# Two transformer blocks on one core: the mixer's head scores issued in pairs, and its remainders as two products

## The chip, the cores and the metric

The kernel runs on one core of a Trainium2 chip. The metric is the device time of one execution in microseconds (us); lower is better. A measurement of this kernel is taken in several runs, and the median is compared.

## What is computed

The reference runs two transformer blocks over 256 tokens of width 1024 in float32. The first block (two layers of differential attention, a Fourier mixer and a gated feed-forward) is untouched. The second block has a feed-forward, then a *mixer*, then another feed-forward. The change lies in the mixer's attention, which is a "stick breaking" attention with 8 heads of width 64:

```python
z = jnp.einsum('bhqd,bhkd->bhqk', q_blk, k_c) * scale
valid = s_pos[None, :] < t_pos[:, None]
sp = jnp.where(valid, jax.nn.softplus(z), 0.0)
rem = lax.cumsum(sp, axis=3, reverse=True) - sp
log_a = jax.nn.log_sigmoid(z) - rem
a = jnp.where(valid, jnp.exp(log_a), 0.0)
outs.append(jnp.einsum('bhqk,bhkd->bhqd', a, v_c))
```

So for each head there are scores `z`, a softplus of them, a "remainder" (a sum over all later keys, made here as a product with a triangle of ones), an exponential, and the product with the values.

## The kernel before

All weights come from memory as a stream of chunks of 128 x 2048 float32 (1 MB). The chunks go through three slots. ScalarE (ACT) rounds a chunk to its high part (`split` in its program, L850), VectorE (DVE) subtracts to get the low part (`split` there, L1195, which signals `lo_ready`), and TensorE (PE) multiplies: each float32 product is three products of high and low parts (L438). In the mixer a projection chunk is 48 such matmuls of 256 columns; `projection(..., ks=range(4 * part, 4 * part + 4))` does one half of a chunk, 24 matmuls.

Each engine runs its own program strictly in the order in which it is written, and waits on semaphores. The order is written by hand. The attention of the mixer is woven into projection chunks 6 to 12. On PE, after each half chunk comes one step for one head: `remainders(h - 2)`, `z_scores(h)`, `values2(h - 4)`. Scores and keys lie with keys on the partitions, 384 columns for each head (256 queries against the first 128 keys, then 128 queries against the second 128 keys). The queries and keys of an even head lie on partitions 0 to 63 and those of the odd head on 64 to 127, so that a score product uses only 64 rows of PE's array (a row group).

For one head the work goes round the engines:

- PE `z_scores(h)` writes the scores to bank 2 or 3 (`z_done`). It waits for `z_read` of head h - 2, which frees the bank.
- ACT `log1p_exp(h)`: Abs (L1127), Exp (L1129) and Ln (L1131) of 128x384. Exp and Ln need different tables, and each change is a table load.
- DVE `softplus(h)`: three operations of 128x384 (L1567, L1571, L1574). The second signals `z_read`, the third `masked_ready`.
- PE `remainders(h)` (waits for `masked_ready`), then DVE `subtract_remainder(h)` (L1580, signals `log_a_ready`), ACT `exp_a(h)` (L1135), DVE `mask_a(h)` (L1585, signals `a2_ready`), and PE `values2(h)` (L782, L784).

ACT and DVE walk through steps `s` = 0 to 12. Before, step s holds the softplus chain of head s - 1 and the exponential of head s - 3. Odd steps also hold the split of chunk 9 + s // 2 and, on DVE, the copy of a finished projection out of its bank (L1626) or a convolution.

Of the kernel before, what the change touches and what calls it, by code (L numbers as in the profile page):

```python
# [30 lines left out]
P = 128  # L31
S = 256
# [3 lines left out]
HEADS = 8  # L36
ATT = 512
HD = 32
VD = 64
# [38 lines left out]
def fused_blocks(nc, x, stream, ada, w_f, layer_params, common_params, rows, consts32, out):  # L78
    with ExitStack() as ctx:
        def sb(name, shape, dt=F32):  # L80
            return ctx.enter_context(nc.sbuf_tensor(name, shape, dt))

        def sem(name):
            return ctx.enter_context(nc.semaphore(name))
# [5 lines left out]
        h = sb("h", [P, 2, D])  # L90
# [26 lines left out]
        def view(n, **dims):  # L117
            at = used[0]
            used[0] += n
            assert used[0] <= WORK  # L120
            return work[:, at:at + n]
# [7 lines left out]
        qT = view(4 * S).rearrange("p (k n) -> p k n", k=4)  # L129
        kT = view(4 * S).rearrange("p (k n) -> p k n", k=4)  # L130
# [30 lines left out]
        tri = c32[:, TRI:TRI + P]  # L161
        ones = c32[:, ONES:ONES + P]
# [22 lines left out]
        B = [banks[:, i, :] for i in range(8)]  # L185
# [87 lines left out]
        z_done = sem("z_done")  # L273
# [3 lines left out]
        z_read = sem("z_read")  # L277
# [152 lines left out]
        def _(pe):  # L430
# [320 lines left out]
            t = MIX_T  # L751
            EV = 8 * DEPTH

            def z_scores(h):

                if h >= 2:
                    pe.wait_ge(z_read, h - 1)
                r = VD * (h % 2)
                q, k = qT[r:r + VD, h // 2, :], kT[r:r + VD, h // 2, :]
                bank = B[2 + h % 2]  # L760
                nc.tensor.matmul(bank[:, 0:S], k[:, 0:P], q, start=True, stop=True, skip_group_check=True)
                nc.tensor.matmul(bank[:, S:S + P], k[:, P:S], q[:, P:S], start=False, stop=True,
                                 skip_group_check=True).then_inc(z_done, 1)

            def remainders(h):

                pe.wait_ge(masked_ready, h + 1)
                if h >= 2:
                    pe.wait_ge(log_a_ready, h - 1)
                bank, sp_ = B[4 + h % 2], soft[h % 3]  # L770
                nc.tensor.matmul(bank[:, 0:S], tri, sp_[:, 0:S], start=True, stop=False, skip_group_check=True)
                nc.tensor.matmul(bank[:, P:S], ones, sp_[:, S:S + P], start=False, stop=True, skip_group_check=True)
                nc.tensor.matmul(bank[:, S:S + P], tri, sp_[:, S:S + P], start=False, stop=True,
                                 skip_group_check=True).then_inc(rem_done, 1)

            def values2(h):
# [13 lines left out]
            for j in range(2, 20):  # L790

                if j < 12:
                    pe.wait_ge(proj_evac, EV + j - 1)
                elif 12 <= j < 14:
                    pe.wait_ge(cx_evac, j - 11)
                elif j >= 14:
                    pe.wait_ge(proj_evac, EV + j - 3)
                if j < 6 or j >= 13:
                    projection(t, j, B[j % 2], x_hi, x_lo)
                    continue  # L800
                for part in range(2):
                    h = 2 * (j - 6) + part
                    projection(t, j, B[j % 2], x_hi, x_lo, ks=range(4 * part, 4 * part + 4))
                    if h == 0:
                        pe.wait_ge(proj_evac, EV + 6)
                    if 2 <= h < HEADS + 2:
                        remainders(h - 2)
                    if h < HEADS:
                        z_scores(h)
                    if 4 <= h < HEADS + 3:  # L810
                        values2(h - 4)
                    if h == HEADS + 4:
                        values2(HEADS - 1)
# [30 lines left out]
        def _(act):  # L844
# [260 lines left out]
            for j in range(6):  # L1105
                act.wait_ge(chunk_done, 3 * t + j + 1)
                bank = B[j % 2][:, :].rearrange("p (m n) -> p m n", m=2)
# [13 lines left out]
            def log1p_exp(h):  # L1121

                act.wait_ge(z_done, h + 1)
                if h >= 2:
                    act.wait_ge(z_read, h - 1)
                buf = remain[:, h % 2, :]
                nc.scalar.activation(buf, B[2 + h % 2][:, 0:384], ACT.Abs).then_inc(soft_step, 1)  # L1127
                act.wait_ge(soft_step, 3 * h + 1)
                nc.scalar.activation(buf, buf, ACT.Exp, scale=-1.0).then_inc(soft_step, 1)  # L1129
                act.wait_ge(soft_step, 3 * h + 2)  # L1130
                nc.scalar.activation(buf, buf, ACT.Ln, bias=1.0).then_inc(soft_step, 1)  # L1131
# [11 lines left out]
                nc.scalar.activation(mix_hi[:, 4 + n, :], conv_y[:, n, :], ACT.Copy).then_inc(conv_hi, 1)  # L1143

            for s in range(13):
                if 1 <= s <= HEADS:
                    log1p_exp(s - 1)
                if 3 <= s < HEADS + 3:
                    exp_a(s - 3)
                if s >= 6 and s % 2 == 0:  # L1150
                    heads_hi((s - 6) // 2)
                if s % 2 == 1:
                    split(t, 6 + s // 2 + 3)
# [37 lines left out]
        def _(dve):  # L1191
            def split(t, j):

                dve.wait_ge(hi_ready, 3 * t + (j + 1))
                nc.vector.tensor_tensor(w_lo[j % SLOTS][:, :], raw[j % SLOTS][:, :],  # L1195
                                        w_hi[j % SLOTS][:, :].bitcast(F32), ALU.subtract).then_inc(lo_ready, 1)
# [364 lines left out]
            def softplus(h):  # L1561

                dve.wait_ge(soft_step, 3 * h + 3)
                if h >= 3:
                    dve.wait_ge(rem_done, h - 2)
                z, small_log = B[2 + h % 2][:, 0:384], remain[:, h % 2, :]
                nc.vector.scalar_tensor_tensor(soft[h % 3], z, 0.0, small_log, ALU.max, ALU.add)\  # L1567
                    .then_inc(soft_raw, 1)
                if h >= 4:
                    dve.wait_ge(o2_done, h - 3)  # L1570
                nc.vector.scalar_tensor_tensor(log_a[:, h % 4, :], z, 0.0, small_log, ALU.min, ALU.subtract)\  # L1571
                    .then_inc(z_read, 1)
                dve.wait_ge(soft_raw, h + 1)
                nc.vector.tensor_tensor(soft[h % 3], soft[h % 3], mask, ALU.mult)\  # L1574
                    .then_inc(masked_ready, 1)
# [16 lines left out]
            def conv(i):  # L1592

                dve.wait_ge(chunk_done, 3 * t + 11 + i)
                dve.wait_ge(proj_evac, 8 * DEPTH + 10)
                nc.vector.tensor_tensor(vpad[:, 2 * i:2 * i + 2, 2:S + 2],
                                        B[i][:, :].rearrange("p (m n) -> p m n", m=2), gate_c[:, 2 * i:2 * i + 2, :],
                                        ALU.mult).then_inc(cx_evac, 1)
                dve.wait_ge(cx_evac, i + 1)
                dve.wait_ge(pads_ready, 1)  # L1600
                for n in (2 * i, 2 * i + 1):
                    y = conv_y[:, n, :]
                    tap = [cp[:, CONV_W + 4 * w + n:CONV_W + 4 * w + n + 1] for w in range(3)]
                    nc.vector.tensor_scalar(y, vpad[:, n, 0:S], tap[0], None, ALU.mult).then_inc(conv_step, 1)
                    for w in (1, 2):
                        dve.wait_ge(conv_step, 4 * n + w)
                        nc.vector.scalar_tensor_tensor(y, vpad[:, n, w:w + S], tap[w], y, ALU.mult, ALU.add)\
                            .then_inc(conv_step, 1)
                    dve.wait_ge(conv_step, 4 * n + 3)
                    nc.vector.tensor_tensor(y, y, gate_b[:, n, :], ALU.mult).then_inc(conv_step, 1)  # L1610

            for s in range(13):
                if 3 <= s < HEADS + 3:
                    subtract_remainder(s - 3)
                if 1 <= s <= HEADS:
                    softplus(s - 1)
                if 3 <= s < HEADS + 3:
                    mask_a(s - 3)
                if s >= 6 and s % 2 == 0:
                    heads_lo((s - 6) // 2)  # L1620
                if s % 2 == 1:
                    j = 6 + s // 2
                    if j < 10:
                        dve.wait_ge(chunk_done, 3 * t + j + 1)
                        out = (gate_b if j < 8 else gate_c)[:, 2 * (j % 2):2 * (j % 2) + 2, :]
                        nc.vector.tensor_copy(out, B[j % 2][:, :].rearrange("p (m n) -> p m n", m=2))\  # L1626
                            .then_inc(proj_evac, 1)
                    else:
                        conv(j - 10)
                    split(t, j + 3)  # L1630
            for n in range(4):
                dve.wait_ge(conv_hi, n + 1)
# [165 lines left out]
```

## Time and profile before

| | |
|---|---|
| median of 3 runs | 1209.72 us (1205.0 to 1209.92) |
| the profiled execution's own time | 1209.38 us |
| its span, first to last instruction | 1207.7 us |
| mean granted clock of TensorE | 0.983 of full speed |
| PE busy | 1168.7 us, 97% |
| DVE busy | 865.5 us, 72% |
| ACT busy | 611.1 us, 51% |

The span is what the trace covers; the execution's own time is 1.7 us longer. Busy shares are averages over the whole program. The mixer's heads take up only the stretch from about 858 to 916 us, and that stretch has to be read by itself. A float32 product of the heads shows as two records of the same matmul (two passes); a product of high and low parts shows as one. Times in a row are given as start and duration, and neighbouring operations overlap by some 0.1 us, so that costs are best read as the distance between starts.

### The profile page before, as it was taken

The numbers are of one execution on the slowest core, as the hardware profiler recorded it, in microseconds if no ns is written. First come the engines' busy times: TensorE is split into PE (matmuls) and PEld (weight loads), VectorE is DVE, ScalarE is ACT, GpSimd is POOL, SyncE is SP. The second block draws the span as 40 slices with busy tenths as digits, with TensorE's granted clock in tenths as the row PEclk, the third lists the DMA queues.
The fourth block names the chain that finished last, engine by engine and source line by source line (L and its number), as shares of the span: only waits on it lengthen the run. The fifth ranks groups of instructions, "written<-read, shape, count | busy, mean of one in ns | idle before, by whom it ended". The sixth has DMA issues, their size and how long they took to land.

```text
span 1207.7 us, 17757 instructions
## 1 busy us (share of the span) xinstructions
PE 1168.7 (97%) x6642; PEld 1007.3 (83%) x6642; DVE 865.5 (72%) x1130; ACT 611.1 (51%) x745; POOL 104.7 (9%) x99
## 2 busy tenths in 40 slices
PE   8998999999999899999979999999999999999997
PEld 7987888887897788888768888878989987888886
DVE  6576878887857787888796788876477367655555
ACT  5674545444557454544444445444795445444443
POOL 2500600000130060000010000000000000000000
PEclk9999999999899999999989999998999998999999
DMA  9612676775342267777546677635424553555550
GB/s 362 238 71 105 229 271 263 298 279 225 139 176 70 105 238 269 263 290 282 222 142 212 255 278 282 264 150 180 170 101 143 177 185 134 201 175 187 195 174 35
DMA packets 34991, 242.62 MB, mean 201 GB/s; under 512 B 3808, under 2 KB 5232, under 8 KB 8448
## 3 DMA queue, kind: packets, MB, share of 16 engines
q1 hardware_dynamic: 28992, 196.56, 43.7%
q0 software_dynamic: 5520, 45.17, 10.2%
q8 instruction: 33, 0.54, 0.2%
q10 hardware_dynamic: 432, 0.24, 0.1%
q14 instruction: 14, 0.11, 0.0%
HBM read 240.90 MB, written 1.05 MB: 200 GB/s over the span
## 4 chain that ended last, share of the span: by engine, by line
PE 83%; DVE 8%; ACT 5%; issue 3%; DMA 0%; POOL 0%; DVEq 0%; SPq 0%; ACTq 0%
PE bank L438 39%; PE bank L471 25%; PE bank L473 13%; ACT w_hi L850 2%; PE bank L625 1%; DVE work L1328 1%; PE bank L602 1%; DVE small L1220 1%; PE bank L578 1%; DVE h L1233 1%; PE bank L615 1%; PE bank L528 1%; PE bank L643 1%; DVE w_lo L1195 0%; DVE h L1253 0%
## 5 line engine op out<-in xcount | busy, mean ns | idle before, releaser
L1195 DVE TENSOR_TENSOR w_lo<-raw,w_hi 128x2048 fp32r<-128x2048 f32 x178 | 414.4, 2330 | 141.4 <-ACT w_hi L850 141.3
L471 PE MATMUL bank<-x_parts,w_hi 128*128 128x512 f32 x1408 | 501.0, 400 | 2.7 <-DVE x_parts L1277 2.3
L473 PE MATMUL bank<-x_parts,w_lo 128*128 128x256 f32 x1408 | 396.2, 281 | 0.0
L850 ACT ACTIVATE w_hi<-raw 128x2048 fp32r<-128x2048 f32 x183 | 349.1, 1908 | 43.3 <-PE bank L438 37.3
L471 PEld LDWEIGHTS bank<-x_parts,w_hi 128*128 128x128 f32 x1408 | 265.7, 189 | 69.7 <-issue 3.5
L473 PEld LDWEIGHTS bank<-x_parts,w_lo 128*128 128x128 f32 x1408 | 267.2, 190 | 1.4
L438 PE MATMUL bank<-x_parts,w_hi 128*128 128x256 f32 x832 | 153.0, 286 | 0.7 <-ACT work L1111 0.7
L438 PE MATMUL bank<-w_hi,hid_hi 128*128 128x512 f32 x352 | 139.3, 396 | 2.8 <-DVE hid_lo L1316 2.8
L438 PE MATMUL bank<-w_lo,hid_hi 128*128 128x512 f32 x352 | 139.1, 395 | 0.0
L438 PE MATMUL bank<-w_hi,hid_lo 128*128 128x512 f32 x352 | 138.8, 394 | 0.0
L438 PEld LDWEIGHTS bank<-x_parts,w_hi 128*128 128x128 f32 x832 | 129.3, 191 | 3.8 <-issue 2.0
L438 PE MATMUL bank<-x_parts,w_lo 128*128 128x256 f32 x416 | 117.5, 283 | 0.0
L1328 DVE SCALAR_TENSOR_TENSOR work<-work,c_act 128x384 f32 x168 | 104.0, 619 | 5.9
L890 ACT ACTIVATE hid_hi<-work 128x512 fp32r<-128x512 f32 x44 | 27.8, 631 | 128.7 <-PE bank L438 114.7
L874 ACT ACTIVATE work<-bank 128x512 f32<-128x512 f32 x44 | 26.3, 598 | 125.7 <-PE bank L473 122.1
L438 PEld LDWEIGHTS bank<-w_hi,hid_hi 128*128 128x128 f32 x352 | 66.0, 187 | 20.0 <-DVE hid_lo L1316 4.1
L438 PEld LDWEIGHTS bank<-x_parts,w_lo 128*128 128x128 f32 x416 | 79.6, 191 | 0.0
L438 PEld LDWEIGHTS bank<-w_hi,hid_lo 128*128 128x128 f32 x352 | 66.0, 187 | 16.0
L438 PEld LDWEIGHTS bank<-w_lo,hid_hi 128*128 128x128 f32 x352 | 66.0, 188 | 14.2
L1316 DVE TENSOR_TENSOR hid_lo<-work,hid_hi 128x512 fp32r<-128x512 f32 x44 | 32.7, 743 | 59.3 <-ACT hid_hi L890 59.3
L438 PE MATMUL bank<-w_hi,x_parts 128*128 128x512 f32 x224 | 72.2, 399 | 2.6 <-DVE x_parts L1277 1.8
L356 POOL TENSOR_TENSOR small<-small 128x1 f32<-128x1 f32 x18 | 11.7, 652 | 532.9 <-DVE small L1259 421.7
(176 smaller groups left out, 1251.7 us busy)
## 6 DMA issues: line engine op xcount, KB each, us to landing
raw<-stream SPq DMA_DIRECT2D x183, 1024.0 KB, 4.8
work<-ada POOLq DMA_DIRECT2D x24, 1536.0 KB, 6.8
gain_rows<-rows POOLq DMA_DIRECT2D x11, 512.0 KB, 5.7
gate_rows<-rows POOLq DMA_DIRECT2D x3, 512.0 KB, 17.5
h<-x SPq DMA_DIRECT2D x4, 256.0 KB, 4.7
raw<-stream SPq DMA_DIRECT2D x2, 512.0 KB, 6.8
out<-z SPq DMA_DIRECT2D x4, 256.0 KB, 2.1
c<-consts SPq DMA_DIRECT2D x1, 962.0 KB, 13.9
```

The lines of the kernel that those rows point to most:

```text
L438: last = nc.tensor.matmul(out, stationary, moving, start=start and i == 0, stop=stop and i == 2, skip_group_check=True)
L471: nc.tensor.matmul(pair[:, n, :], wh[:, k, cols], x_parts[:, k, :, :].rearrange("p a n -> p (a n)"), start=k == 0, stop=False, skip_group_ ...
L473: last = nc.tensor.matmul(pair[:, n, 0:S], wl[:, k, cols], x_hi[:, k, :], start=False, stop=k == KT - 1, skip_group_check=True)
L528: last = nc.tensor.transpose(XT[k // 2][:, k % 2 * S + m * P:k % 2 * S + (m + 1) * P], z[:, m, k * P:(k + 1) * P], ident)
L578: last = nc.tensor.matmul(B[1][:, q:q + 1], ada_acc[:, q * P:(q + 1) * P], ones[:, 0:1], start=True, stop=True, skip_group_check=True)
L602: last = nc.tensor.matmul(SCORES[u][:, m * S:(m + 1) * S], qT[r:r + HD, p, m * P:(m + 1) * P], kT[r:r + HD, p, :], start=True, stop=True, ...
L850: nc.scalar.activation(w_hi[j % SLOTS][:, :], raw[j % SLOTS][:, :], ACT.Copy).then_inc(hi_ready, 1)
L874: nc.scalar.activation(gate_rest.rearrange("p (a n) -> p a n", a=2), GATE[:, :, S:2 * S], ACT.Copy)\
L890: nc.scalar.activation(out[:, :, :].rearrange("p k n -> p (k n)"), hidden, ACT.Copy)\
L1195: nc.vector.tensor_tensor(w_lo[j % SLOTS][:, :], raw[j % SLOTS][:, :], w_hi[j % SLOTS][:, :].bitcast(F32), ALU.subtract).then_inc(lo_ready, 1)
L1316: nc.vector.tensor_tensor(lo[:, :, :].rearrange("p k n -> p (k n)"), hidden, hi[:, :, :].rearrange("p k n -> p (k n)").bitcast(F32), ALU.s ...
L1328: nc.vector.scalar_tensor_tensor(acc, ada_raw[:, k, :], c_act[:, k:k + 1], acc, ALU.mult, ALU.add).then_inc(ada_step, 1)
```

## The change

On PE the scores of heads 2p and 2p + 1 are issued together after the first half of a chunk, in the order: even head 256 columns, odd head 256 columns, even head 128, odd head 128. The pair waits for `z_read` of both heads of the pair before it. After the second half of a chunk no scores are issued. The three products of a remainder (256, 128 and 128 columns) become two (384 and 128 columns). ACT runs the Abs, Exp and Ln of both heads of a pair one after the other in odd steps, and nothing of them in even steps. DVE does the softplus of the even head where it stood in odd steps, and that of the odd head at the end of the same step, just ahead of the split.

```diff
-            def z_scores(h):
-
-                if h >= 2:
-                    pe.wait_ge(z_read, h - 1)
-                r = VD * (h % 2)
-                q, k = qT[r:r + VD, h // 2, :], kT[r:r + VD, h // 2, :]
-                bank = B[2 + h % 2]
-                nc.tensor.matmul(bank[:, 0:S], k[:, 0:P], q, start=True, stop=True, skip_group_check=True)
-                nc.tensor.matmul(bank[:, S:S + P], k[:, P:S], q[:, P:S], start=False, stop=True,
-                                 skip_group_check=True).then_inc(z_done, 1)
+            def z_scores(pair):
+
+                if pair >= 1:
+                    pe.wait_ge(z_read, 2 * pair)
+                q, k = ([part[VD * u:VD * (u + 1), pair, :] for u in range(2)] for part in (qT, kT))
+                for u in range(2):
+                    nc.tensor.matmul(B[2 + u][:, 0:S], k[u][:, 0:P], q[u], start=True, stop=True,
+                                     skip_group_check=True)
+                for u in range(2):
+                    nc.tensor.matmul(B[2 + u][:, S:S + P], k[u][:, P:S], q[u][:, P:S], start=False, stop=True,
+                                     skip_group_check=True).then_inc(z_done, 1)
...
-                nc.tensor.matmul(bank[:, 0:S], tri, sp_[:, 0:S], start=True, stop=False, skip_group_check=True)
-                nc.tensor.matmul(bank[:, P:S], ones, sp_[:, S:S + P], start=False, stop=True, skip_group_check=True)
-                nc.tensor.matmul(bank[:, S:S + P], tri, sp_[:, S:S + P], start=False, stop=True,
+                nc.tensor.matmul(bank[:, 0:S + P], tri, sp_[:, 0:S + P], start=True, stop=False, skip_group_check=True)
+                nc.tensor.matmul(bank[:, P:S], ones, sp_[:, S:S + P], start=False, stop=True,
                                  skip_group_check=True).then_inc(rem_done, 1)
...
-                    if h < HEADS:
-                        z_scores(h)
+                    if h < HEADS and part == 0:
+                        z_scores(h // 2)
...
             for s in range(13):
-                if 1 <= s <= HEADS:
+                if s % 2 == 1 and s < HEADS:
                     log1p_exp(s - 1)
+                    log1p_exp(s)
...
                 if 3 <= s < HEADS + 3:
                     subtract_remainder(s - 3)
-                if 1 <= s <= HEADS:
+                if s % 2 == 1 and s < HEADS:
                     softplus(s - 1)
...
                     else:
                         conv(j - 10)
+                    if s < HEADS:
+                        softplus(s)
                     split(t, j + 3)
```

On VectorE, the place is step 5 of its walk. Before, the rows run from the softplus of head 4, over the mask of head 2, the copy of chunk 8 and the split of chunk 11, to the remainder of head 3 and the softplus of head 5 in step 6:

```order
L1567 SCALAR_TENSOR_TENSOR work<-bank,work 128x384 [waits rem_done,soft_step]
L1571 SCALAR_TENSOR_TENSOR work<-bank,work 128x384 [waits o2_done]
L1574 TENSOR_TENSOR work<-work,c 128x384 [waits soft_raw]
L1585 TENSOR_TENSOR work<-work,c 128x384 [waits a_exp_ready]
L1626 COPY work<-bank 128x512 [waits chunk_done]
L1195 TENSOR_TENSOR w_lo<-raw,w_hi 128x2048 [waits hi_ready]
L1580 TENSOR_TENSOR work<-work,bank 128x384 [waits z_read,rem_done]
L1567 SCALAR_TENSOR_TENSOR work<-bank,work 128x384 [waits rem_done,soft_step]
L1571 SCALAR_TENSOR_TENSOR work<-bank,work 128x384 [waits o2_done]
L1574 TENSOR_TENSOR work<-work,c 128x384 [waits soft_raw]
```

After, the same place (line numbers are one higher here):

```order
L1568 SCALAR_TENSOR_TENSOR work<-bank,work 128x384 [waits rem_done,soft_step]
L1572 SCALAR_TENSOR_TENSOR work<-bank,work 128x384 [waits o2_done]
L1575 TENSOR_TENSOR work<-work,c 128x384 [waits soft_raw]
L1586 TENSOR_TENSOR work<-work,c 128x384 [waits a_exp_ready]
L1627 COPY work<-bank 128x512 [waits chunk_done]
L1568 SCALAR_TENSOR_TENSOR work<-bank,work 128x384 [waits rem_done,soft_step]
L1572 SCALAR_TENSOR_TENSOR work<-bank,work 128x384 [waits o2_done]
L1575 TENSOR_TENSOR work<-work,c 128x384 [waits soft_raw]
L1196 TENSOR_TENSOR w_lo<-raw,w_hi 128x2048 [waits hi_ready]
L1581 TENSOR_TENSOR work<-work,bank 128x384 [waits z_read,rem_done]
```

The odd head's three operations moved from behind the split and the subtraction to a place ahead of both, but behind the mask of an older head.

On ScalarE, the place is the same pair of heads. Before, from the exponential of head 1 over the logarithm chain of head 4, the exponential of head 2 and the split to the chain of head 5:

```order
L1135 ACTIVATE work<-work 128x384 [waits log_a_ready]
L1127 ACTIVATE work<-bank 128x384 [waits z_read,z_done]
L1129 ACTIVATE work<-work 128x384 [waits soft_step]
L1131 ACT_TABLE_LOAD
L1131 ACTIVATE work<-work 128x384 [waits soft_step]
L1135 ACT_TABLE_LOAD
L1135 ACTIVATE work<-work 128x384 [waits log_a_ready]
L850 ACTIVATE w_hi<-raw 128x2048 [waits chunk_done,raw_landed2]
L1127 ACTIVATE work<-bank 128x384 [waits z_read,z_done]
L1129 ACTIVATE work<-work 128x384 [waits soft_step]
L1131 ACT_TABLE_LOAD
L1131 ACTIVATE work<-work 128x384 [waits soft_step]
```

After, from the exponential of head 1 to the split:

```order
L1135 ACTIVATE work<-work 128x384 [waits log_a_ready]
L1127 ACTIVATE work<-bank 128x384 [waits z_read,z_done]
L1129 ACTIVATE work<-work 128x384 [waits soft_step]
L1131 ACT_TABLE_LOAD
L1131 ACTIVATE work<-work 128x384 [waits soft_step]
L1127 ACTIVATE work<-bank 128x384 [waits z_read,z_done]
L1129 ACT_TABLE_LOAD
L1129 ACTIVATE work<-work 128x384 [waits soft_step]
L1131 ACT_TABLE_LOAD
L1131 ACTIVATE work<-work 128x384 [waits soft_step]
L1135 ACT_TABLE_LOAD
L1135 ACTIVATE work<-work 128x384 [waits log_a_ready]
```

Both chains of logarithms now stand in one run, and the split of the weights (L850) comes only after them and the exponential of head 2.

## Rows read from the trace of the kernel before

**Rows 1.** The page, part 1: engine, busy us (share), instructions.

```profile
PE 1168.7 (97%) x6642; PEld 1007.3 (83%) x6642; DVE 865.5 (72%) x1130; ACT 611.1 (51%) x745; POOL 104.7 (9%) x99
```

**Rows 2.** Busy time by stretch: start:end, length, busy per engine, PEclk, DMA share, GB/s.

```profile
859.00:904.00 45.00, 44.44 (x311) 39.75 (x310) 30.79 (x45) 43.86 (x53) 0.00 (x0) 1.00 0.29 99
921.00:981.00 60.00, 60.00 (x502) 60.00 (x502) 30.89 (x23) 26.91 (x28) 0.00 (x0) 1.00 0.55 193
```

**Rows 3.** Waits of PE between 857 and 921 us: total, times, longest.

```profile
PE bank L771 <- DVE work L1574: 0.6, 1, 0.6
```

**Rows 4.** Timeline of PE, 862 to 868 us: start, us, what; scores, then remainder.

```profile
862.24 0.28 PE L438 MATMUL bank<-x_parts,w_lo 128*128 128x256 f32 x1
862.45 0.70 PE L761 MATMUL bank<-work 64*128 64x256 f32 x2
862.98 0.38 PE L762 MATMUL bank<-work 64*128 64x128 f32 x2
863.29 0.50 PE L438 MATMUL bank<-x_parts,w_hi 128*128 128x256 f32 x2
...
866.26 0.60 PE L771 MATMUL bank<-work,c 128*128 128x256 f32 x2
...
867.23 0.70 PE L761 MATMUL bank<-work 64*128 64x256 f32 x2
```

**Rows 5.** Timeline of PE at 51 us: scores of the first block, four row groups.

```profile
51.19 1.15 PE L602 MATMUL bank<-work 32*128 32x256 f32 x16
```

**Rows 6.** Timeline of ACT, 886 to 904 us.

```profile
886.31 1.90 ACT L850 ACTIVATE w_hi<-raw 128x2048 fp32r<-128x2048 f32 x1
888.11 0.47 ACT L1127 ACTIVATE work<-bank 128x384 f32<-128x384 f32 x1
...
889.15 1.28 ACT L1131 ACT_TABLE_LOAD   x1
890.45 0.53 ACT L1131 ACTIVATE work<-work 128x384 f32<-128x384 f32 x1
890.99 1.28 ACT L1135 ACT_TABLE_LOAD   x1
892.28 0.53 ACT L1135 ACTIVATE work<-work 128x384 f32<-128x384 f32 x1
892.72 0.37 ACT L1139 ACTIVATE mix_hi<-bank 128x256 fp32r<-128x256 f32 x1
...
897.59 1.90 ACT L850 ACTIVATE w_hi<-raw 128x2048 fp32r<-128x2048 f32 x1
...
903.57 0.52 ACT L1135 ACTIVATE work<-work 128x384 f32<-128x384 f32 x1
```

**Rows 7.** Timeline of DVE; in brackets the idle time ahead and its releaser.

```profile
863.68 0.56 DVE L1567 SCALAR_TENSOR_TENSOR work<-bank,work 128x384 f32<-128x384 f32 x1 [3.19 <-ACT work L1131]
...
886.43 0.56 DVE L1585 TENSOR_TENSOR work<-work,c 128x384 f32<-128x384 f32 x1 [0.35 <-ACT work L1135]
886.91 0.68 DVE L1626 COPY work<-bank 128x512 f32<-128x512 f32 x1
888.23 2.29 DVE L1195 TENSOR_TENSOR w_lo<-raw,w_hi 128x2048 fp32r<-128x2048 f32 x1 [0.64 <-ACT w_hi L850]
890.44 0.55 DVE L1580 TENSOR_TENSOR work<-work,bank 128x384 f32<-128x384 f32 x1
891.00 0.56 DVE L1567 SCALAR_TENSOR_TENSOR work<-bank,work 128x384 f32<-128x384 f32 x1
891.48 0.55 DVE L1571 SCALAR_TENSOR_TENSOR work<-bank,work 128x384 f32<-128x384 f32 x1
```

**Rows 8.** Stretches around three long waits of PE; PEclk stands before the last two numbers.

```profile
112.00:115.20 3.20, 0.50 (x3) 0.07 (x1) 3.06 (x7) 0.00 (x0) 0.68 (x2) 0.97 0.00 0
115.00:118.40 3.40, 3.12 (x14) 2.84 (x15) 2.95 (x6) 1.40 (x4) 0.63 (x1) 0.50 0.00 0
413.60:420.00 6.40, 2.23 (x17) 1.68 (x16) 5.82 (x13) 1.93 (x4) 0.79 (x1) 1.00 0.00 0
612.00:618.00 6.00, 0.47 (x5) 0.38 (x4) 5.23 (x12) 1.39 (x4) 1.54 (x2) 0.61 0.01 1
618.00:623.60 5.60, 4.88 (x20) 4.30 (x21) 4.80 (x15) 2.86 (x6) 1.71 (x3) 0.50 0.56 142
```

## The prediction

> **What bounds the kernel now.** I read the page first, then the stretches, then the waits, and last the timelines of the three engines. The page says that PE is busy for 97% of the span [rows 1], so nearly every microsecond of PE's work counts, and every microsecond that it waits counts too. In the stretch of the heads, 859 to 904 us, PE is busy for 44.44 of 45 us, but ACT is busy for 43.86 of 45 as well [rows 2]. Two engines are full at once there. PE's only wait is 0.6 us, for the masked softplus of head 7 [rows 3]. After it, from 921 to 981 us, PE is full without a gap while DVE and ACT are half idle [rows 2]: what is lost in the heads can't be won back there.
>
> ACT's rows give its period. The split at 886.31 is followed by the next one at 897.59, so one chunk with two heads takes ACT 11.28 us [rows 6]. PE's period for the same work can't be longer than that, since it never falls behind. So before the change each engine has hardly a microsecond in hand per chunk, and the order decides.
>
> **What PE saves.** The last projection matmul ahead of a score step starts at 862.24, the scores at 862.45, and projection goes on at 863.29 [rows 4]. Projection matmuls start 0.12 us apart (48 of them are one chunk of 5.76 us), so a score step costs 863.29 - 862.24 - 0.12 = 0.93 us, and about 0.1 more because the first matmul behind it starts slowly (two records in 0.50 where 0.40 is usual). In the first block 16 passes of 256 columns in four row groups take 1.15 us together [rows 5]; one pass alone takes 0.21 (the second halves of the 0.53 from 862.45 to 862.98), so they overlap. I therefore take a pair of heads at the price of one, and PE loses four steps of about 1.03: 4.1 us less. The bounds: if the pair doesn't overlap at all it streams four products in a row, 0.64 us more a pair, and the saving is 1.6 us; if it overlaps fully, 4.1.
>
> The remainder streams 256 + 128 + 128 = 512 columns before and 384 + 128 = 512 after. From 866.26 to 867.23 it takes 0.97 [rows 4], which is 512 columns at 0.21 us a pass of 256, twice, plus the change to 64 rows. Nothing of that is taken away. I cost it at 0, between 0 and 0.1 us a head less, and since it lies inside waits (below) either end gives 0.
>
> **What moves on ACT and DVE.** No operation is added. The table loads stay 17, since in the new order too each Ln and nearly each Exp finds the other's table. But two queues are reordered. ACT does both logarithm chains, then an exponential, then the split. DVE does softplus of the even head, then `mask_a`, then the copy, then softplus of the odd head, then the split, and only then `subtract_remainder`. Three waits follow.
>
> *The first pair.* Head 0's logarithm ends as before, and its softplus starts at 863.68 [rows 7]. The chain of head 1 takes Abs 0.50, load 1.29, Exp 0.55, load 1.29, Ln 0.53 = 4.1 us [rows 6], so it ends at 867.7. `z_read` comes with DVE's second operation, 0.47 + 0.55 later [rows 7], at 868.8. PE, without the step at 862.45, is through half a chunk (2.97) and remainder 0 (0.88) at 863.29 - 0.93 + 3.85 = 866.2. The next scores need `z_read` of head 1: a wait of 2.6 us.
>
> *The second pair.* Scores at 868.8, Abs 0.95 later at 869.7, two chains of 4.05 and 0.1 for the load behind end at 877.9, and the exponential of head 0 (load 1.29, Exp 0.52) at 879.8. Only now can DVE do `mask_a(0)` (0.48), the copy (0.60) and two operations of softplus(3) (1.02): `z_read` at 881.9. PE has done two half chunks, remainders 1 and 2 and a score step, 0.85 + 2.97 + 0.97 + 2.87 + 0.88 = 8.5, and stands at 877.3: a wait of 4.6 us.
>
> *The loop.* From here ACT and DVE hold each other. DVE can't start the split before softplus(odd) is done, and `subtract_remainder(odd)` stands behind the split; ACT needs it for `exp_a(odd)`, ahead of the next chains. One turn: load and exponential of the even head 1.72 [rows 6]; then until DVE is through mask, copy and softplus, 0.12 + 0.48 + 0.60 + 1.41 = 2.6; split on DVE 2.21; subtraction 0.58 (the last two from 888.23, 890.44 and 891.00 [rows 7]); `exp_a(odd)` 0.43 (892.28 to 892.72 [rows 6]); two chains 2.76 + 4.17 = 6.93, the first without a load for Exp. Sum 14.5 us against 11.28 before, with ACT idle for 3.6 of it. PE isn't in this sum at all: it can't speed it up.
>
> By this turn `exp_a(1)` starts at 885.1, `exp_a(3)` at 899.5 and `exp_a(5)` at 914.2. Before, `exp_a(5)` started at 903.57 [rows 6]. It feeds `values2(5)`, the last step of PE that waits; from there both kernels have the same work on a full PE. The delay is 914.2 - 903.57 = **10.7 us**.
>
> The cross-check from PE's side: its waits become 2.6 + 4.6 + 4.3 (third pair) + 3.0 (`values2(4)` for `mask_a(4)`) + 1.0 (`remainders(7)` for `subtract_remainder(5)`) + 0.2 = 15.7 us, less the 0.6 of before and the 4.1 saved = 11.0. The two agree within the rounding.
>
> The splits come later too, by 4 to 11 us, but PE reaches the chunks as late as they do. The split of chunk 9 ends at 871.8 and PE starts chunk 9 at 888. The stream's DMAs follow the splits and have as long.
>
> Sum: 1209.38 us of the profiled execution + 10.7 = 1220.1. This execution lies 0.3 under the median of the three runs, so I forecast 1220.4 as a median.
>
> **The rivals.** *The clock falls in the new waits.* After a wait before 115.28 PE's granted clock was 0.50 (1.2 GHz) for 3.4 us, with about 2.7 us idle ahead; around 413.6 to 420, with PE busy for only 2.23 of 6.40 us, it stayed at 1.00 (2.4 GHz); after nearly 6 us of idle it was 0.50 up to 623.6 [rows 8]. The new waits of 4.6 and 4.3 us lie between. A fall behind the first three waits is swallowed by the next wait. Behind the last long one (3.0) half speed for 3.4 us costs 1.7, of which the two small waits behind take 1.2, and for a longer fall of 10 us up to 1.6 more remains than they take. That gives 1221 to 1222.5, and 1224 if the pair doesn't overlap either.
>
> The Trainium skill, page "TensorE: Matmul & The Clock Gate", section "Why this matters for your kernels", speaks against waits of this size: it asks for no long idle gaps between bursts of matmuls, since PE then drops to its half clock. By that rule each of the three waits over 4 us or near it is followed by slow matmuls, and the time is that of this rival. This case's trace agrees after two waits and not after a third.
>
> *The pair doesn't overlap* (the change doesn't do what it says). For: these groups have 64 rows and only two run side by side, where the trace shows four of 32. Then each pair is 0.64 us longer. ACT waits that much longer for the first pair and for the second, since it has nothing else to do there; the third and fourth lie inside ACT's other work. So the whole train comes 1.3 us later: 1220.1 + 1.3 = 1221.4.
>
> *Faster: the loop doesn't bind.* If a turn took less than PE's own period, about 11.28 - 1.0 = 10.3 us, only the saving would be left: 1209.4 - 4.1 = 1205.3. For it: PE's busy share. Against it: the turn is 14.5 by rows, and its largest parts (chains 6.93, split 2.21) have the same duration in every row. It would need 4.2 us to drop out of the turn, that is, that DVE subtracts ahead of the split, which its order excludes.
>
> *The rest of the program shifts.* Clock falls elsewhere [rows 8] depend on where in time PE's gaps lie, and a shift of 10.7 us moves them. The three runs differ by 4.9 us. If such a difference falls to the good side the result is about 1214.5.
>
> **How the numbers follow.** Waits as worked out, clock kept or its fall swallowed: 0.60, 1218.5 to 1222. Clock falls that cost: 0.17, 1221 to 1224. No overlap: 0.05. The shifted rest, lower by up to 5: 0.12, of which about half ends within 0.5% of before. Faster: 0.06. A measurement of this kernel can tell about 0.5% (6 us) from no change. So faster 0.05, same 0.08, slower 0.87. The range holds the first four cases but for the edges: 1214.5 to 1224.5.
>
> **What the profile would show.** Right: PE's row for the scores names `z_read` (DVE's second softplus operation) as releaser of waits of about 2.6, 4.6 and 4.3 us; ACT's exponential of an odd head is preceded by 3.6 us idle for the subtraction three times; splits on ACT are 14.5 us apart; a pair of scores takes about 0.85 us. Wrong: if ACT is still full in 859 to 904, or if the waits are there but the scores' pair takes 1.5 us, or if PE waits at other steps (for `lo_ready`, which I cost at nothing), the steps above fail one by one.

## The result, and the profile after

The changed kernel takes 1219.55 us (median of 6 runs, 1215.95 to 1220.48), the kernel before 1208.97 us (median of its 6 runs, 1205.0 to 1210.02). The ratio is 1.0087, with a 95% interval of 1.0068 to 1.0106: slower by 0.9%, 10.6 us. The profiled execution took 1219.33 us with a span of 1217.6 us; forecast were 1220.4.

The waits of PE between 850 and 940 us, which answer to [rows 3], in the changed kernel (line numbers: L760 scores, L772 remainder, L782 values; L1572, L1581 and L1586 are DVE's second softplus operation, the subtraction and the mask):

```profile
PE bank L760 <- DVE work L1572: 9.6, 3, 4.1
PE bank L772 <- DVE work L1581: 0.8, 1, 0.8
PE bank L782 <- DVE work L1586: 0.7, 1, 0.7
```

Where PE waited 0.6 us, it now waits 11.1 in all. The five waits in the timeline of PE, with the idle time and its releaser in brackets:

```profile
869.32 0.70 PE L760 MATMUL bank<-work 64*128 64x256 f32 x4 [2.45 <-DVE work L1572]
...
882.51 0.70 PE L760 MATMUL bank<-work 64*128 64x256 f32 x4 [3.09 <-DVE work L1572]
...
896.98 1.23 PE L760 MATMUL bank<-work 64*128 64x256 f32 x4 [4.09 <-DVE work L1572]
...
910.19 0.65 PE L782 MATMUL bank<-work 128*64 128x256 f32 x2 [0.67 <-DVE work L1586]
...
914.94 0.88 PE L772 MATMUL bank<-work,c 128*128 128x384 f32 x2 [0.82 <-DVE work L1581]
```

What held them up is in ACT's timeline, over one turn from split to split, which answers to [rows 6]:

```profile
880.24 1.89 ACT L850 ACTIVATE w_hi<-raw 128x2048 fp32r<-128x2048 f32 x1
885.62 0.53 ACT L1135 ACTIVATE work<-work 128x384 f32<-128x384 f32 x1 [3.49 <-DVE work L1581]
886.05 0.48 ACT L1127 ACTIVATE work<-bank 128x384 f32<-128x384 f32 x1
...
894.71 1.89 ACT L850 ACTIVATE w_hi<-raw 128x2048 fp32r<-128x2048 f32 x1
```

ACT has nothing to do for 3.49 us after its split, until DVE has subtracted the remainder of an odd head. From split to split it is 14.47 us, and the next turn, which also holds ACT's operation on a finished pair of heads (L1139), takes 14.74 (to the split at 909.45). Before, these two turns took 11.01 and 11.28 (splits at 875.30, 886.31 and 897.59), so each grew by 3.46 us, just about ACT's wait. DVE's timeline in the same turn, to be read against [rows 7], shows why:

```profile
880.36 0.56 DVE L1586 TENSOR_TENSOR work<-work,c 128x384 f32<-128x384 f32 x1 [4.40 <-ACT work L1135]
880.84 0.68 DVE L1627 COPY work<-bank 128x512 f32<-128x512 f32 x1
881.44 0.55 DVE L1568 SCALAR_TENSOR_TENSOR work<-bank,work 128x384 f32<-128x384 f32 x1
881.90 0.55 DVE L1572 SCALAR_TENSOR_TENSOR work<-bank,work 128x384 f32<-128x384 f32 x1
882.37 0.55 DVE L1575 TENSOR_TENSOR work<-work,c 128x384 f32<-128x384 f32 x1
882.83 2.29 DVE L1196 TENSOR_TENSOR w_lo<-raw,w_hi 128x2048 fp32r<-128x2048 f32 x1
885.04 0.55 DVE L1581 TENSOR_TENSOR work<-work,bank 128x384 f32<-128x384 f32 x1
```

DVE idles 4.40 us for the mask of an old head, although the logarithm of the new odd head (it starts at 877.97 and takes 0.52 us) has been done since 878.5. Behind that mask stand the copy, the softplus that frees PE's bank, the split, and last the subtraction that ACT waits for. So in each turn ACT waits 3.49 us for DVE, and DVE 4.40 us for ACT (besides shorter waits of 0.59 and 1.75 us).

The stretches, as in [rows 2], show the loss (PE busy 35.37 of 45 us where it was 44.44), and that PE is full again behind it:

```profile
859.00:904.00 45.00, 35.37 (x234) 30.94 (x234) 24.43 (x36) 36.30 (x44) 0.00 (x0) 0.89 0.28 97
...
931.70:991.70 60.00, 60.00 (x503) 60.00 (x502) 31.06 (x23) 27.47 (x28) 0.00 (x0) 1.00 0.54 193
```

To compare kernels I use one length, the *head stage*: from the start of the first score product to the start of the last values product, by the timeline of PE. Before it runs from 858.54 to 915.97, 57.4 us. After:

```profile
859.05 0.70 PE L760 MATMUL bank<-work 64*128 64x256 f32 x4
859.58 0.39 PE L763 MATMUL bank<-work 64*128 64x128 f32 x4
...
927.07 0.38 PE L784 MATMUL bank<-work 128*64 128x128 f32 x2
```

That is 68.0 us, 10.6 more. The span grew by 9.9 only: 0.5 us more ahead of the stage, and 1.2 less behind it, in a part that isn't changed. There, between 1000 and 1025 us, the mean granted clock was 0.86 in the profiled execution of before and 1.00 in this one.

The first of these rows also shows the pair: four passes of 256 columns in 0.70 us, as long as two passes of one head took in [rows 4], and projection goes on at 859.90, 0.85 us after the pair's start.

### The profile page after: what moved, and what is told of

The parts are those of the page before. It is cut to its first block, busy times and chain, and to the rows that moved or that the text cites. A ratio compares the mean times of both kernels' runs of the same rounds, so it can differ in the third digit from the quotient of the medians.

```text
span 1217.6 us, 17725 instructions
## 1 busy us (share of the span) xinstructions
PE 1165.2 (96%) x6626; PEld 1002.1 (82%) x6626; DVE 861.9 (71%) x1130; ACT 611.3 (50%) x745; POOL 104.8 (9%) x99
## 4 chain that ended last, share of the span: by engine, by line
PE 82%; DVE 9%; ACT 5%; issue 3%; DMA 0%; POOL 0%; DVEq 0%; SPq 0%; ACTq 0%
PE bank L438 39%; PE bank L471 25%; PE bank L473 12%; PE bank L625 1%; DVE w_lo L1196 1%; DVE work L1329 1%; ACT w_hi L850 1%; PE bank L602 1%; DVE small L1221 1%; PE bank L578 1%; DVE x_parts L1278 1%; ACT L1129 1%; DVE h L1234 1%; PE bank L528 1%; ACT work L995 1%
## 5 line engine op out<-in xcount | busy, mean ns | idle before, releaser
L850 ACT ACTIVATE w_hi<-raw 128x2048 fp32r<-128x2048 f32 x183 | 349.2, 1908 | 42.3 <-PE bank L438 36.5
```

The costliest lines, as they stand in the source:

```text
L850: nc.scalar.activation(w_hi[j % SLOTS][:, :], raw[j % SLOTS][:, :], ACT.Copy).then_inc(hi_ready, 1)
```

## The experiments

The head stage can be read to better than 0.1 us and is free of the rest of the program, so it stands beside each ratio. It comes from one execution of each kernel, though, and a fall of the clock in that execution is part of it; the ratio and its interval come from all runs. Nine more kernels ran; the table is followed by each of them. The expectations call "queue theory" the prediction's account: the price is set by what stands ahead of the awaited operations in the queues of ACT and DVE.

| kernel | head stage, us | against before | ratio to before | interval |
|---|---|---|---|---|
| before | 57.43 | | 1 | |
| changed | 68.02 | +10.6 | 1.0087 | 1.0068 to 1.0106 |
| remainder alone | 57.43 | 0.0 | 0.9996 | 0.9981 to 1.0010 |
| pair on PE alone | 62.92 | +5.5 | 1.0042 | 1.0026 to 1.0057 |
| order on ACT and DVE alone | 68.76 | +11.3 | 1.0091 | 1.0070 to 1.0113 |
| changed, PE kept busy in waits | 68.40 | +11.0 | 1.0075 | 1.0055 to 1.0096 |
| changed, subtraction first | 62.93 | +5.5 | 1.0052 | 1.0033 to 1.0071 |
| changed, chains interleaved | 57.96 | +0.5 | 1.0004 | 0.9992 to 1.0015 |
| changed, DVE reordered | 59.75 | +2.3 | 1.0029 | 1.0013 to 1.0046 |
| both of these | 53.93 | -3.5 | 0.9980 | 0.9965 to 0.9994 |
| both, scores head by head | 72.93 | +15.5 | 1.0126 | 1.0102 to 1.0150 |

**The remainder alone.** Only the diff's lines on the three products, on the kernel before.

```diff
-                nc.tensor.matmul(bank[:, 0:S], tri, sp_[:, 0:S], start=True, stop=False, skip_group_check=True)
-                nc.tensor.matmul(bank[:, P:S], ones, sp_[:, S:S + P], start=False, stop=True, skip_group_check=True)
-                nc.tensor.matmul(bank[:, S:S + P], tri, sp_[:, S:S + P], start=False, stop=True,
+                nc.tensor.matmul(bank[:, 0:S + P], tri, sp_[:, 0:S + P], start=True, stop=False, skip_group_check=True)
+                nc.tensor.matmul(bank[:, P:S], ones, sp_[:, S:S + P], start=False, stop=True,
...
```

> The remainder as two products alone, everything else as before. Queue theory: the same 512 columns, no change, within 0.3 us. Rival, a 384-column product is dearer (or cheaper) than 256 and 128: more than 0.1 us for each of 8 heads, so about 1 us or more either way.

The stage is unchanged to 0.1 us, and the interval of the ratio holds 1. No cost and no gain of this part can be seen.

**The pair on PE alone.** `z_scores(pair)` and its call as in the change; ACT, DVE and the remainder as before.

```diff
-                    if h < HEADS:
-                        z_scores(h)
+                    if h < HEADS and part == 0:
+                        z_scores(h // 2)
```

> Pair of scores on PE alone: ACT and DVE keep the order of the kernel before, the remainder keeps its three products. Queue theory (the cost is the order on ACT and DVE, which makes one turn 14.5 us instead of 11.3): that turn stays at 11.3, but the first pairs must wait for z_read of an odd head, 4.4 us at pair 1, 4.0 at pair 2, 1.1 at pair 3, less about 4 saved on PE: +4 to +5 us over before. Rival, the pairing itself costs (the wait for two heads): the whole +10.6. Rival, clock: as much as the granted clock falls in these waits, so near +10 too.

PE's waits for the pair:

```profile
869.97 1.22 PE L760 MATMUL bank<-work 64*128 64x256 f32 x4 [4.24 <-DVE work L1572]
...
883.32 0.70 PE L760 MATMUL bank<-work 64*128 64x256 f32 x4 [1.91 <-DVE work L1572]
...
894.68 0.70 PE L760 MATMUL bank<-work 64*128 64x256 f32 x4 [0.95 <-DVE work L1572]
```

That pairing sets the whole price falls: the pair by itself costs half of it, +5.5, and by waits that die out (4.24, 1.91, 0.95), since ACT's turn stays short. It is 0.5 to 1.5 more than the 4 to 5 worked out. In this run the granted clock was 0.50 for 6.8 us from 869.5, just when the pair was issued; it took 1.22 us for its first products instead of 0.70, and ACT, which had nothing else to do, started on the scores 1.68 us after the pair (at 871.65) instead of 0.96 as in the changed kernel (869.32 to 870.28). So about 0.7 us of the excess can be put down to the clock; that is read from rows, not from a run of its own. The fall also ate into the second wait, worked out as 4.0.

**The order on ACT and DVE alone.** PE as before, the loops of ACT and DVE as in the change:

```diff
             for s in range(13):
-                if 1 <= s <= HEADS:
+                if s % 2 == 1 and s < HEADS:
                     log1p_exp(s - 1)
+                    log1p_exp(s)
...
+                    if s < HEADS:
+                        softplus(s)
                     split(t, j + 3)
```

> The new order on ACT and DVE alone: PE issues scores head by head and three products a remainder, as before. Queue theory: the turn is 14.5 us whatever PE does, with ACT idle 3.6 us ahead of exp_a of heads 1, 3 and 5; PE waits at other steps (values2 of heads 0, 2, 4 for mask_a, remainders 3, 5, 7 for the subtraction, about 2.7, 2.4, 3.5 and three times 1.0): +10 to +10.5 us over before. Rival, pairing: about 0, since no pair waits. Rival, clock: waits are smaller than 4 us, so the clock stays at 2.4 GHz and less is lost, under +6.

The whole loss is here without any pair, +11.3 us. ACT's waits for the subtraction between 858 and 930 us are those of the changed kernel:

```profile
ACT work L1135 <- DVE work L1581: 17.3, 5, 5.7
```

PE waits at other steps, for masks (2.35, 1.09 and 3.30 us ahead of the values) and once for the subtraction (0.83). So it isn't PE's wait for two heads that sets the price, but the turn of ACT and DVE; PE mostly just shows it wherever it next needs a result.

It is 0.8 us over the upper end of the +10 to +10.5 worked out, and the rival's condition, that the clock stays up in waits under 4 us, did not hold: the granted clock was 0.50 for 6.8 us from 880.4, around the end of the wait of 2.35, and for 3.4 us from 911.1, behind the one of 3.30. After the first fall began, ACT waited for scores from PE, which was late by it, and that turn took 15.17 us (split at 880.04 to split at 895.21):

```profile
889.30 0.49 ACT L1127 ACTIVATE work<-bank 128x384 f32<-128x384 f32 x1 [0.59 <-PE bank L762]
```

So in this run PE did enter the turn once. What share of the 0.8 us comes from the falls was not tested.

**PE kept busy in the waits.** The changed kernel, with filler products ahead of the wait.

```diff
+            FILL = {1: 18, 2: 34, 3: 32}
...
                 if pair >= 1:
+                    for _ in range(FILL[pair]):
+                        nc.tensor.matmul(B[7][:, 0:S], ones_r[:, :], x_hi[:, 0, :], start=True, stop=True,
+                                         skip_group_check=True)
                     pe.wait_ge(z_read, 2 * pair)
```

> The changed kernel, with PE kept busy inside its three waits for z_read: 18, 34 and 32 matmuls of 256 columns on data that is never used, into a bank that nobody reads then, just ahead of the waits. Queue theory: falls of the clock are swallowed by the next wait, so the time stays that of the changed kernel, within 1 us, with the granted clock at 1.00 through 859 to 915. Rival, clock: a good part of the 10.6 us comes back (4 us or more).

The filler takes up 10.65 us, the three waits shrink to 0.33, 0.58 and 0.32 us, the clock stays at 1.00 through all of them, and the stage is no shorter, 68.4. Head 5's exponential on ACT starts 55.77 us after the first scores (914.49 - 858.72), and did so after 55.78 without filler (914.83 - 859.05). Without the filler the clock had fallen twice:

```profile
871.00:874.40 3.40, 3.40 (x19) 3.40 (x18) 1.80 (x2) 3.36 (x5) 0.00 (x0) 0.50 0.26 48
...
894.90:901.70 6.80, 4.72 (x20) 3.60 (x21) 6.21 (x10) 3.28 (x5) 0.00 (x0) 0.50 0.13 23
```

So these falls cost nothing: what PE lost by them it would have waited. The expectation that the clock would stay at 1.00 up to 915 failed: this run had a fall of 3.4 us at another place, from 910.6, behind an unfilled wait of 2.82 us. As ACT's part was on time, the 0.4 us more is what PE lost at the lower clock and no later wait took up:

```profile
909.85 0.65 PE L787 MATMUL bank<-work 128*64 128x256 f32 x2 [2.82 <-DVE work L1591]
910.34 0.40 PE L789 MATMUL bank<-work 128*64 128x128 f32 x2
910.66 0.80 PE L438 MATMUL bank<-x_parts,w_hi 128*128 128x256 f32 x2
```

**The subtraction first.** The changed kernel with one DVE operation moved ahead of the split.

```diff
             for s in range(13):
-                if 3 <= s < HEADS + 3:
+                if s % 2 == 1 and 3 <= s < HEADS + 3:
                     subtract_remainder(s - 3)
...
                     if s < HEADS:
                         softplus(s)
+                    if 3 <= s < HEADS + 3:
+                        subtract_remainder(s - 2)
                     split(t, j + 3)
```

> The changed kernel with one DVE operation moved: the subtraction of the remainder of an odd head goes ahead of the split in the odd step, instead of behind it. Queue theory: the split (2.2 us) leaves the turn, ACT's wait ahead of exp_a(odd) falls from 3.5 to 1.4 us and the turn to 12.3; PE waits 2.6, 4.6, 2.1, 0.8 and 0.5: +5.6 us over before instead of +10.6. Rivals (pairing, clock): the waits of the pairs stay, no more than 1 us comes back.

Moving one operation of 0.55 us per pair brings back 5.1 us of 10.6. ACT's rows in the turn:

```profile
878.19 1.89 ACT L850 ACTIVATE w_hi<-raw 128x2048 fp32r<-128x2048 f32 x1
881.37 0.52 ACT L1135 ACTIVATE work<-work 128x384 f32<-128x384 f32 x1 [1.28 <-DVE work L1581]
...
890.45 1.89 ACT L850 ACTIVATE w_hi<-raw 128x2048 fp32r<-128x2048 f32 x1
```

The wait is 1.28 instead of 3.49 us and the turn 12.26 instead of 14.47: 2.21 less each, which is what the split takes on DVE. The split was in the loop.

**Chains interleaved.** The changed kernel; ACT does Abs of both heads, then Exp of both, then Ln of both (`at` counts `soft_step`, and DVE's softplus waits for step 5 or 6 of the pair).

```diff
-            def log1p_exp(h):
+            def log1p_exp(p):
...
+                at = 6 * p
+                pair = (2 * p, 2 * p + 1)
+                bufs = [remain[:, h % 2, :] for h in pair]
...
+                for u in range(2):
+                    act.wait_ge(soft_step, at + 1 + u)
+                    nc.scalar.activation(bufs[u], bufs[u], ACT.Exp, scale=-1.0).then_inc(soft_step, 1)
+                for u in range(2):
+                    act.wait_ge(soft_step, at + 3 + u)
+                    nc.scalar.activation(bufs[u], bufs[u], ACT.Ln, bias=1.0).then_inc(soft_step, 1)
...
-                dve.wait_ge(soft_step, 3 * h + 3)
+                dve.wait_ge(soft_step, 6 * (h // 2) + 5 + h % 2)
```

> The changed kernel with ACT's two chains interleaved: Abs, Abs, Exp, Exp, Ln, Ln, so that a pair has one load of each table less. Queue theory: 2 loads of 1.28 us a turn less, so the turn is 11.9 instead of 14.5 while ACT's wait ahead of exp_a(odd) stays 3.5: +1.4 us over before, about -9 against the changed kernel. If instead table loads were not in the turn (hidden in waits), it would stay at +10.

This alone undoes the loss, to +0.5 us and a ratio of 1.0004. The two turns that took 14.47 and 14.74 us now take 11.48 and 11.76 (splits at 875.80, 887.28 and 899.04), with ACT still idle for 3.5 in each. Between 858 and 920 us ACT does 9 table loads where it did 17. The turn is 0.4 us shorter than the two loads saved would make it, for the most part because two Abs now take 0.74 us up to the first Exp (881.61 to 882.35), where a single one took 0.51 (886.05 to 886.56 in the changed kernel). The stage came out 0.9 under the +1.4 worked out, and the shorter turns point to the reason.

**DVE reordered, and both together.** On DVE an odd step now has both subtractions, both softplus and both masks ahead of the copy and the split; even steps keep only `heads_lo`.

```diff
...
                 if 3 <= s < HEADS + 3:
                     subtract_remainder(s - 3)
-                if s % 2 == 1 and s < HEADS:
+                if s < HEADS:
                     softplus(s - 1)
                 if 3 <= s < HEADS + 3:
+                    subtract_remainder(s - 2)
+                if s < HEADS:
+                    softplus(s)
+                if 3 <= s < HEADS + 3:
                     mask_a(s - 3)
...
+                    mask_a(s - 2)
...
```

On top of the changed kernel alone:

> The changed kernel with the same new DVE order as the run before this, but ACT's chains one after the other with all their table loads. Queue theory: ACT has no wait in the turn and is the bound at 10.9 us a turn, PE waits 2.6, 1.7, 0.5, 0.2, 0.5 and 1.8: +2.4 us over before. Rivals (pairing, clock): +8 or more.

Together with the interleaved chains:

> As the run with interleaved chains, and on DVE both softplus, both subtractions and both masks of a step stand ahead of the copy and the split. Queue theory: neither the split nor the mask of an old head stands ahead of z_read or log_a any more; the turn falls under PE's own 10.3 us, PE waits only 1.0 and 0.4 us, and its saved score steps show: -3.5 us against before. If pairing costs by itself, it can't get under before.

The reordering alone gives +2.3 us, with +2.4 worked out. PE's second wait was 0.19 us where 1.7 was worked out: the granted clock was 0.50 for 3.4 us from 867.0, which made PE some 1.5 us later, and the wait took that up as in the changed kernel. Both edits together give -3.5, as worked out, without any fall in the stage, and the ratio is 0.9980 (0.9965 to 0.9994). That is under the kernel before, and under the changed one by 14.1 us in the stage and by some 13 us in the ratios. PE's waits in the stage of this run:

```profile
PE bank L772 <- DVE work L1579: 0.6, 1, 0.6
PE bank L760 <- DVE work L1576: 0.3, 1, 0.3
```

ACT is now busy for 35.76 us of 45 in the stretch 859 to 904, where it was 43.86 [rows 2], and the score steps that PE saves show in the time.

**Both, but scores head by head.** As the last run, with `z_scores(h)` of the kernel before on PE.

> The run with interleaved chains and the new DVE order, but PE issues the scores head by head again (remainders stay two products). Queue theory: interleaved chains need both heads' scores at once, and the odd head's come half a chunk later, so ACT waits about 4 us ahead of the second Abs of each pair and PE waits for the masked softplus at remainders 0 and 2 (3.3 each) and 4 and 6 (1.2 each): +10 us over before, 13 more than with pairs. Rival, the gain of the run with pairs came from ACT's saved table loads alone, whatever PE does: it stays 1 us or more under before.

The stage is 72.9 us, +15.5: interleaved chains without paired scores are the worst of all, and the rival that saved table loads alone bring the gain is ruled out. The direction is the queue theory's; the size is 5.5 us over its +10. The granted clock points to where the rest may come from, two falls of 6.8 us each:

```profile
866.50:873.30 6.80, 5.86 (x18) 4.62 (x19) 5.54 (x8) 2.07 (x2) 0.00 (x0) 0.50 0.10 18
883.60:890.40 6.80, 6.80 (x25) 5.14 (x24) 5.58 (x8) 2.85 (x4) 0.00 (x0) 0.50 0.00 0
```

```profile
876.93 0.49 ACT L1129 ACTIVATE work<-bank 128x384 f32<-128x384 f32 x1 [5.31 <-PE bank L762]
...
893.76 0.49 ACT L1129 ACTIVATE work<-bank 128x384 f32<-128x384 f32 x1 [6.97 <-PE bank L762]
```

Here ACT waits for PE's odd head. In the four pairs it waits 3.41, 5.31, 6.97 and 4.49 us, where about 4 each was worked out, and the two longest waits (from 871.62 and 886.79) begin inside the two falls. So PE at its lower clock is in the chain. PE was busy for 5.86 and 6.80 us in the falls. By the projection matmuls it loses 44% of such time (in the changed kernel they start 0.21 us apart in a fall and 0.12 otherwise), and by products that only stream columns up to half. That makes 5.5 to 6.3 us, about the 5.5 to be explained. That a fall costs this much was not tested by a run of its own; it is inferred from these rows.

## Why the prediction was right, point by point

*What bounds the kernel.* Right: both PE and ACT were full, and nothing behind the stage gave the loss back ([rows 2], and the stretch from 931.7 us after, where PE is full).

*What PE saves.* Right, close to the end of the range that I took: the pair takes 0.85 us as one head did. It shows as time only where no wait stands in its place, in the run with interleaved chains and reordered DVE. There the stage is 3.5 us shorter with 0.9 us of waits against 0.6 before, so the saving was 3.8 us, a little under the 4.1 that I had put.

*The remainder at 0.* Right, by a run of its own.

*The loop.* Right: 14.5 us worked out, 14.47 measured (the turn to set beside it is the one of 11.01 before, not that of 11.28); ACT's idle time 3.6 worked out and 3.49 measured, at heads 1, 3 and 5. The run with the order alone shows that the pair isn't needed for it, the run with filler that PE's speed isn't in it in the changed kernel, and the run with the subtraction first that the split is.

*The size.* +10.7 us forecast, 10.6 measured in the stage. (The two starts that the prediction subtracts, 914.2 and 903.57, give 10.63; it wrote 10.7. The time forecast, 1220.4 us, lies 0.9 over the 1219.55 measured, since it started from 1209.72, the median of three runs, where that of six is 1208.97.) Head 5's exponential, from which the delay was taken, came 10.75 us later, counted from the first scores. One link was named wrongly: PE did not wait for the values of head 5. Its last wait was 0.82 us for the subtraction one operation ahead (L1581, at 914.25), which stands in the same chain. An agreement to 0.1 us is partly luck, since it needs the falls of the clock to land where a wait takes them up: the same kind of sum was off by 0.5 to 1.5 us for the pair alone, by 0.8 to 1.3 for the order alone, by 0.9 for the interleaved chains and by 5.5 for the last run.

*PE's single waits.* Partly off. Worked out were 2.6, 4.6, 4.3, 3.0, 1.0 and 0.2, together 15.7; measured were 2.45, 3.09, 4.09, 0.67 and 0.82, together 11.1. Missing is what two falls of the clock made PE slower: it was busy for 3.40 and 4.72 us at the lower clock. At 0.21 us a projection matmul instead of 0.12 the first fall cost it 1.5 us, and the second, at half speed in the scores and values, up to 2.4. The second and the fourth wait fell short by 1.5 and 2.3. The cross-check from PE's side needed this term; the sum along ACT and DVE did not.

*The rival of the clock.* It fell twice, and cost nothing in the changed kernel, since the next wait took it: the run with filler shows it. As a mechanism for the 10.6 us it is ruled out. The page "TensorE: Matmul & The Clock Gate" of the Trainium skill asks in "Why this matters for your kernels" for no idle gaps over about 3 us between bursts of matmuls. The trace agrees with it at the wait of 4.09 us, and not at the one of 3.09, after which the clock stayed, nor at the one of 2.45, after which it fell. Such a fall cost nothing here; where ACT waited for PE, in the last run, the rows point to some 5 us.

*Another rival, pairing without overlap,* is ruled out by the pair's row. *Faster* would have needed a turn under PE's own period. The run with both edits has that: its turn of 9.97 us from split to split (882.43 to 892.40) holds 1.70 us in which ACT waits for PE's scores, so there PE sets the pace.

The order itself is a two-part matter. Pairing on PE, with the old order behind it, costs 5.5 us; the new order, with the old PE program, 11.3; both together 10.6. The parts don't add, since both are waits for the same two queues. What stays open is how much each further fall of the clock is worth in runs other than the profiled one: the runs of one kernel differ by some 5 us, and only one execution of each has rows.

## What to carry to other kernels

When two in-order engines pass results to each other, add up one full turn through both queues, with everything that stands ahead of each awaited operation, and compare it with the bound engine's period: that sum told the time of this change to 0.1 us, and that of eight of the nine other kernels to within 1.5, while the busy shares and the saving on the bound engine told nothing. It goes wrong where an engine in the turn slows down, as PE did in the last run. An operation that another engine waits for goes ahead of long work that nobody waits for yet (here 0.55 us moved ahead of a 2.2 us split was worth 5 us), and no operation that has to wait goes ahead of one that is ready (the whole new order on DVE was worth 3 us more than that one move). And when work is grouped in pairs, group it on every engine in the way that saves something (here one table load of each of the two kinds saved per pair), or the pair only adds latency.

## What the runs showed of the hardware

Two products of 64 rows in different row groups ran side by side at no cost: with the records taken singly, the passes of the two heads start 6 or 7 ns apart, 859.046 and 859.052 for the first, and the pair took 0.85 us, where one head took 0.84 (862.45 to 863.29 [rows 4]).

The length of one wait doesn't tell whether the granted clock falls to 0.50 (1.2 GHz). It fell after 2.45 us of idle in the changed kernel (from 871.0, when PE had been working again since 869.3), and at the same wait of 2.46 us in two other runs (subtraction first, DVE reordered). It didn't fall at the wait of 3.09 us, in the changed kernel or with the subtraction first. Its price hangs on who waits for PE: nothing in the changed kernel, and by rows alone about 0.7 us in the run with the pair alone.

A change of ACT's table cost 1.29 us: the load takes 1.28 us, and the next ACTIVATE starts 1.29 us after the load did (887.10 to 888.39 in the changed kernel). Two such changes fewer, 2.6 us, are most of the 3.0 us by which a turn is shorter with interleaved chains.
